# Half of the modulation's chunks moved from VectorE to TensorE, and two column groups taken in turn

## The reference, cut to what matters

```python
def rmsnorm(x, g):
    xf = x.astype(jnp.float32)
    y = xf * lax.rsqrt(jnp.mean(xf * xf, axis=-1, keepdims=True) + EPS)
    return (y * g.astype(jnp.float32)).astype(x.dtype)
...
    c_act = jax.nn.silu(c)
    for l in range(DEPTH):
        mod = c_act @ w_ada[l] + b_ada[l]
        sh1, sc1, gt1, sh2, sc2, gt2 = jnp.split(mod[:, None, :], 6, axis=-1)
        h = rmsnorm(x, g_mix[l]) * (1.0 + sc1) + sh1
        x = x + gt1 * hybrid_mixer(h, w_in[l], ...)
```

## Time and profile before

| what | value |
|---|---|
| median of three runs | 3170.58 us (3169.29 to 3181.39) |
| the profiled execution, its own time | 3177.1 us |
| its span | 3175.3 us |
| mean granted share of TensorE's clock | 0.981 |
| TensorE busy | 3067.2 us (97%) |
| VectorE busy | 2004.9 us (63%) |
| ScalarE busy | 1482.3 us (47%) |
| moved by DMA | 658.41 MB, mean 207 GB/s |

### The profile page before, as it was taken

The page is one execution under the profiler, slowest core; times in us unless marked ns, Lnnn a source line. Parts: engine busy times, 40 slices in busy tenths (PEclk is TensorE's granted clock), DMA queues, the critical chain, the costliest instruction groups (busy, mean ns, idle before and its releaser), DMA issues.

```text
span 3175.3 us, 38367 instructions
## 1 busy us (share of the span) xinstructions
PE 3067.2 (97%) x14170; PEld 2544.3 (80%) x14170; DVE 2004.9 (63%) x2098; ACT 1482.3 (47%) x1740; POOL 107.4 (3%) x206
## 2 busy tenths in 40 slices
PE   6389999999999999999999999999999999999999
PEld 5278777788888888888888888888888888888887
DVE  6879778785656556766555565646575565565564
ACT  4145445544544444555445435544445454444543
POOL 1211110100000000000000000000000000000000
PEclk9689999999999999999999999999999999999999
DMA  9878777685555555555555545555555556545555
GB/s 342 319 301 329 277 272 290 255 295 186 182 194 187 190 187 183 173 174 177 182 183 185 193 153 185 179 188 180 177 175 169 193 171 194 179 156 196 167 185 191
DMA packets 179987, 658.41 MB, mean 207 GB/s; under 512 B 20080, under 2 KB 20368, under 8 KB 179216
## 3 DMA queue, kind: packets, MB, share of 16 engines
q1 hardware_dynamic: 150992, 550.51, 51.7%
q0 software_dynamic: 28864, 106.08, 9.1%
HBM read 654.41 MB, written 2.10 MB: 207 GB/s over the span
## 4 chain that ended last, share of the span: by engine, by line
PE 94%; DVE 3%; DMA 2%; issue 1%; ACT 0%; SPq 0%; DVEq 0%; ACTq 0%
PE pg L1004 29%; PE pg L1006 29%; PE pg L1005 29%; PE pm L1039 2%; DVE R L1597 1%; DMA w_raw<-w 1%; PE pm L1058 1%; DMA R<-w_ada 1%; PE pm L1476 1%; PE pm L1071 0%; PE pm L1370 0%; PE pm L1114 0%; PE pm L1113 0%; DVE w_lo L1675 0%; PE pm L1154 0%
## 5 line engine op out<-in xcount | busy, mean ns | idle before, releaser
L1525 DVE TENSOR_TENSOR w_lo<-w_raw,w_hi 128x1024 fp32r<-128x1024 f32 x888 | 1086.2, 1225 | 974.2 <-ACT w_hi L482 969.6
L482 ACT ACTIVATE w_hi<-w_raw 128x1024 fp32r<-128x1024 f32 x888 | 941.4, 1060 | 1337.7 <-PE pg L1006 1321.6
L1004 PE MATMUL pg<-w_hi,hT_hi 128*128 128x512 f32 x3232 | 1280.2, 396 | 47.2 <-DVE w_lo L1675 34.4
L1006 PE MATMUL pg<-w_hi,hT_lo 128*128 128x512 f32 x3232 | 1265.2, 391 | 0.0
L1005 PE MATMUL pg<-w_lo,hT_hi 128*128 128x512 f32 x3232 | 1264.7, 391 | 0.0
L1004 PEld LDWEIGHTS pg<-w_hi,hT_hi 128*128 128x128 f32 x3232 | 611.6, 189 | 176.3 <-issue 42.9
L1006 PEld LDWEIGHTS pg<-w_hi,hT_lo 128*128 128x128 f32 x3232 | 610.8, 189 | 128.8
L1005 PEld LDWEIGHTS pg<-w_lo,hT_hi 128*128 128x128 f32 x3232 | 612.0, 189 | 124.2 <-issue 0.5
L1004 PE MATMUL pg<-w_hi,y_parts 128*128 128x512 f32 x864 | 337.9, 391 | 1.4 <-issue 1.4
L1006 PE MATMUL pg<-w_hi,y_parts 128*128 128x512 f32 x864 | 336.3, 389 | 0.0
L1005 PE MATMUL pg<-w_lo,y_parts 128*128 128x512 f32 x864 | 336.1, 389 | 0.0
(11 more groups left out here) (270 smaller groups left out, 1383.7 us busy)
## 6 DMA issues: line engine op xcount, KB each, us to landing
w_raw<-w SPq DMA_DIRECT2D x1028, 512.0 KB, 3.5
R<-w_ada POOLq DMA_DIRECT2D x196, 512.0 KB, 5.9
R<-mem_T SPq DMA_DIRECT2D x4, 512.0 KB, 9.4
x_rows<-x SPq DMA_DIRECT2D x1, 2048.0 KB, 20.6
R<-mem_T SPq DMA_DIRECT2D x1, 2048.0 KB, 10.2
out<-x_rows SPq DMA_DIRECT2D x4, 512.0 KB, 5.2
con_sb<-con SPq DMA_DIRECT2D x1, 1344.0 KB, 7.3
small_w_sb<-small_w POOLq DMA_DIRECT2D x2, 576.0 KB, 5.4
```

What stands on the lines that cost most here:

```text
L482: act.activation(w_hi[:, g % RING, :, :].rearrange("p c n -> p (c n)"), raw[:, g % RING, :], ACT.Copy).then_inc(hi_done, 1)
L1004: pe.matmul(out, hi, w_hi[:, slot, c, :], start=start, stop=False)
L1006: return pe.matmul(out, lo, w_hi[:, slot, c, :], start=False, stop=stop)
L1525: tt(flat(w_lo[:, g % RING, :, :]), raw[:, g % RING, :], flat(w_hi[:, g % RING, :, :]).bitcast(F32), ALU.subtract).then_inc(lo_done, 1)
```

## The change

1. In `CHUNKS` the halves 0 and 1 take turns chunk by chunk, and then the halves 2 and 3. The two shift halves (1 and 3, `PE_HALVES`) are not weighed on VectorE: TensorE multiplies each chunk with silu(c) and accumulates in `pm[3]` (`mod_sums`), beginning with the bias. Since 16 products of 8 columns are added in the bank, `ada_sums` isn't needed for them. POOL waits for the engine that used chunk i - 5.
2. Tiles 0 to 7: VectorE weighs two chunks of half 0 after each w_lo, TensorE takes two of half 1 after each tile. Tiles 8 to 23: one chunk of half 2 and one of half 3 a tile. Later halves are weighed from tile 24 on.
3. Tiles 16 to 31: x takes four tiles (input blocks 0 to 7), y four, then x the other four and y the other four.
4. The row norm stands after tile 6's share on VectorE and ScalarE instead of 9; `rows_T` stands between tiles 7 and 10, in three banks. The constants' first part (128 KB) is loaded ahead of the memory's tokens. The forget gate's product comes after tile 27. Many later places in the three programs move by one to four tiles.

```diff
+F_X, F_Y = FRONT.index("x"), FRONT.index("y")
+F_TILES = [(u, j) for u in range(F_X) for j in range(GT)]
+F_TILES += [(u, j) for first in (0, GT // 2) for u in (F_X, F_Y) for j in range(first, first + GT // 2)]
+F_TILES += [(u, j) for u in range(F_Y + 1, F_OUT) for j in range(GT)]
...
+PE_HALVES = (1, 3)
+CHUNKS = [(h, k) for a in (0, 2) for k in range(KD) for h in (a, a + 1)]
+CHUNKS += [(h, k) for h, (q, _) in enumerate(HALVES) if h > 3 for k in range(-1 if q in (2, 5) else 0, KD)]
+DVE_HALVES = [h for h in range(len(HALVES)) if h not in PE_HALVES]
...
             sp.dma_start(vec[:, :], t["vec"]).then_inc(vec_in, 16)
+            sp.dma_start(con[:, 0:2 * P], t["con"][:, 0:2 * P]).then_inc(con_in, 16)
...
                 if i >= ADA_RING:
-                    pool.wait_ge(ada_used, i - ADA_RING + 1)
+                    by_pe = CHUNKS[i - ADA_RING][0] in PE_HALVES
+                    pool.wait_ge(ada_pe if by_pe else ada_used, chunks_before(i - ADA_RING + 1, by_pe))
...
+            act.wait_ge(tile_used, 2 * GT)
             for p in range(4):
                 if p == 2:
-                    upto(22)
+                    upto(26)
                 act.wait_ge(hm_ready, p + 1)
...
+            def mod_sums(h, k):
+
+                i = chunk_at(h, k)
+                q, e = HALVES[h]
+                at = VEC["b_ada"][0] + q * KD + e * (AH // P)
+                out = pm[3][:, 0:AH // P]
+                if k == 0:
+                    if h != PE_HALVES[0]:
+                        pe.wait_ge(mod_taken, 1)
+                    pe.matmul(out, ident, vec[:, at:at + AH // P], start=True, stop=False)
+                pe.wait_ge(ada_in[i % ADA_RING], 16 * (i // ADA_RING + 1))
+                for m in range(AH // P):
+                    last = pe.matmul(out[:, m:m + 1], ada_ring[:, i % ADA_RING, m * P:(m + 1) * P],
+                                     c_act[:, k:k + 1], start=False, stop=k == KD - 1 and m == AH // P - 1)
+                last.then_inc(ada_pe, 1)
...
+            for t in range(8):
+                upto(t + 1)
+                mod_sums(1, 2 * t)
+                mod_sums(1, 2 * t + 1)
+                if t == 7:
+                    pe.wait_ge(rows_ready, 1)
+                    rows_T(0, 0, xn_1)
+                    rows_T(0, 1, xn_1)
+            for t in range(8, 16):
+                upto(t + 1)
+                mod_sums(3, t - 8)
+                if t <= 10:
+                    for q in range(2 * (t - 7), 2 * (t - 7) + 2):
+                        if q >= 3:
+                            pe.wait_ge(hf_done, q - 2)
+                        rows_T(0, q, xn_1)
+            pe.wait_ge(hf_done, GT)
+            ada_sums(0, 0)
             pe.wait_ge(hn_ready, 1)
-            pe.wait_ge(hf_done, GT)
-            transposes(mk_tok[0], (2, 3), T_ps)
-            upto(16)
-            ada_sums(0, 0)
-            ada_sums(1, 1)
-            upto(20)
+            transposes(mk_tok[0], (1, 2), T_ps)
+            for t in range(16, 24):
+                upto(t + 1)
+                mod_sums(3, t - 8)
             pe.wait_ge(mod_taken, 2)
             ada_sums(2, 0)
-            ada_sums(3, 1)
-            upto(24)
+            upto(28)
...
-            weighs = {16 + 6 + i: (4 + i // KD, i % KD) for i in range(6 * KD)}
-            weighs.update({i: (0, i) for i in range(KD)})
+            weighs = {16 + 8 + i: [(4 + i // KD, i % KD)] for i in range(6 * KD)}
+            weighs.update({i: [(0, 2 * i), (0, 2 * i + 1)] for i in range(8)})
+            weighs.update({8 + i: [(2, i)] for i in range(KD)})
...
-            upto(13)
+            upto(11)
+            take_mod(1, 3)
+            upto(14)
             mem_heads(0)
-            upto(20)
-
-            for k in range(KD):
-                weigh(1, k)
-                if k == 3:
-                    take_mod(0, 0)
-            take_mod(1, 1)
+            upto(16)
+            take_mod(0, 0)
             scale_gain(16, V("g_mix")[:, 0:8], 2)
             dve.wait_ge(hf_done, GT)
             modulated(0)
             modulated(1)
-            for k in range(2):
-                weigh(2, k)
+            upto(17)
             lower_4(P_MIX, hf_1)
             lower_4(P_MIX + 1, hf_1)
-            for k in range(2, KD):
-                weigh(2, k)
-            for k in range(KD):
-                weigh(3, k)
-                if k == 3:
-                    take_mod(2, 0)
-                if k in (4, 9):
-                    upto(21 + k // 9)
+            upto(24)
+            take_mod(2, 0)
             take_mod(3, 1)
             scale_gain(24, V("g_mix")[:, 8:16], 4)
             modulated(2)
             modulated(3)
+            upto(26)
             lower_4(P_MIX + 2, hf_1)
             lower_4(P_MIX + 3, hf_1)
```

More of the change, by code:

```diff
@@ L51 @@
 F_OUT = FRONT.index("o0")
-F_TILES = [(u, j) for u in range(F_OUT) for j in range(GT)]
+F_X, F_Y = FRONT.index("x"), FRONT.index("y")
+F_TILES = [(u, j) for u in range(F_X) for j in range(GT)]
+F_TILES += [(u, j) for first in (0, GT // 2) for u in (F_X, F_Y) for j in range(first, first + GT // 2)]
+F_TILES += [(u, j) for u in range(F_Y + 1, F_OUT) for j in range(GT)]
 F_TILES += [(F_OUT + n, j) for n in range(2) for j in range(6)]
@@ L62 @@
 HALVES = ((1, 0), (0, 0), (1, 1), (0, 1), (4, 0), (3, 0), (2, 0), (2, 1), (4, 1), (3, 1), (5, 0), (5, 1))
-CHUNKS = [(h, k) for h, (q, _) in enumerate(HALVES) for k in range(-1 if q in (2, 5) else 0, KD)]
+PE_HALVES = (1, 3)
+CHUNKS = [(h, k) for a in (0, 2) for k in range(KD) for h in (a, a + 1)]
+CHUNKS += [(h, k) for h, (q, _) in enumerate(HALVES) if h > 3 for k in range(-1 if q in (2, 5) else 0, KD)]
+DVE_HALVES = [h for h in range(len(HALVES)) if h not in PE_HALVES]
 IN2 = 15
@@ L399, in chunks_used, with chunks_before, turn @@
         def chunks_used(h):
-            return sum(1 for i, _ in CHUNKS if i <= h)
+            return sum(1 for i, _ in CHUNKS if i <= h and i not in PE_HALVES)
+        def chunks_before(i, by_pe):
+            return sum(1 for h, _ in CHUNKS[:i] if (h in PE_HALVES) == by_pe)
+        def turn(h):
+            return DVE_HALVES.index(h)
         P_MEM0, P_MIX, P_Y, P_MEM1, P_FF = 0, 4, 8, 16, 24
@@ L420, in _ @@
                 if g == 3:
-                    sp.dma_start(con[:, 0:2 * P], t["con"][:, 0:2 * P]).then_inc(con_in, 16)
                     sp.dma_start(x[:, :, :], t["x"]).then_inc(x_in, 16)
@@ L632, in _ @@
             act.activation(spl[:, 0:4], spl[:, 0:4], ACT.Ln, bias=1.0).then_inc(lam_out, 1)
-            upto(9)
+            upto(6)
             act.wait_ge(x_in, 16)
             squares(0, sq_1)
-            upto(13)
+            for q in range(GT):
+                upto(11 + q // 3)
+                rows_T(0, q, hf_1, False)
+            upto(14)
             head_std(0, 8)
-            for q in range(GT):
-                upto(14 + q // 2)
-                rows_T(0, q, hf_1, False)
-            upto(19)
-            heads_T(0, (2, 3), mk_T[:, 0, :, :], scale=V("mk_g")[:, 0:1])
-            upto(20)
+            upto(17)
+            heads_T(0, (1, 2), mk_T[:, 0, :, :], scale=V("mk_g")[:, 0:1])
+            upto(18)
+            act.wait_ge(tile_used, 2 * GT)
             for p in range(4):
                 if p == 2:
-                    upto(22)
+                    upto(26)
                 act.wait_ge(hm_ready, p + 1)
@@ L672, in _ @@
             for gate, (dst, bias) in enumerate(((GR, "ba"), (GI, "bi"))):
-                upto(40 + 3 * gate)
+                upto(43 + 3 * gate)
                 act.wait_ge(lru_ps, gate + 5)
@@ L1070, in ada_sums @@
                 for m in range(AH // P):
-                    i = pe.matmul(pm[bank][:, m:m + 1], ada_acc[h % 2][:, m * P:(m + 1) * P], ones[:, 0:1],
+                    i = pe.matmul(pm[bank][:, m:m + 1], ada_acc[turn(h) % 2][:, m * P:(m + 1) * P], ones[:, 0:1],
                                   start=True, stop=True)
                 i.then_inc(acc_read, 1)
+            def mod_sums(h, k):
[12 more added lines that the diff above has]
+                last.then_inc(ada_pe, 1)
             def broadcast(h, bank):
@@ L1078, in broadcast @@
                 for n in range(2):
-                    i = pe.matmul(pm[bank + n][:, :], ones, ada_acc[h % 2][:, n * NW:(n + 1) * NW], start=True,
+                    i = pe.matmul(pm[bank + n][:, :], ones, ada_acc[turn(h) % 2][:, n * NW:(n + 1) * NW], start=True,
                                   stop=True)
@@ L1175, in _ @@
             for gate in range(2):
-                upto(36 + 3 * gate)
+                upto(39 + 3 * gate)
                 pe.wait_ge(lru_act, 2 + 2 * gate)
@@ L1235, in _ @@
             y_T(1, o1)
-            upto(105)
+            upto(107)
             ada_sums(8, 0)
-            upto(117)
+            upto(119)
             ada_sums(9, 1)
@@ L1676, in upto @@
                        flat(w_hi[:, g % RING, :, :]).bitcast(F32), ALU.subtract).then_inc(lo_done, 1)
-                    if g in weighs:
```

(6 more changed lines are left out.)

96 lines of the change are left out of this document (47 added, 49 removed).

## The result

The changed kernel is slower: 3201.12 us, median of four runs (3196.8 to 3201.9), beside 3174.32 us for the kernel before in the same turns. The ratio is 1.0071, its 95% interval 1.0049 to 1.0093. Measured again in later turns, it was 1.0065 (1.0046 to 1.0084). By these ratios 21 to 23 us are lost (27 by the two medians), more than the 0.5% that I took for the limit of no change.

What follows compares the result with a forecast made beforehand. VectorE's 48 chunks outside the tile loop were taken to stall TensorE about 29 + 34 us. Stages summed to 216.0 us at tile 28 against 206.6, taken as +10 on the median 3170.6: 3181 us, range 3160 to 3204.

Steps and rivals of the forecast that it cites:

- likeliest case: The forecast's own case, chance 0.46: 3181 us, by itself 3172 to 3190, with tiles 0 to 7 ending at 89 us.
- the clock returns late: Rival, chance 0.27: most wide stretches of tiles 0 to 7 end before the clock rises, 11 us a tile, time 3204.
- the sum up to tile 28: Stages added until TensorE is ready for tile 28: 216.0 us against 206.6 before, 9.4 later, taken as +10.
- tiles 0 to 7: A tile and two chunks on TensorE, half the time at each clock level: 8.15 us, times 8 is 65.2.
- The wait for 3.7 us at tile 6: TensorE's earlier idle time, 39.4 to 43.1 us, as tile 6 landed late; kept at 3.7 since the transfers stay.
- The constants, 0.3 us: Loading con's 128 KB ahead of the memory tokens: 0.3 us of transfer, costed at nothing; first matmul at 20.2.
- The bank wait: In tiles 8 to 15, mod_sums(3, 0) waits for VectorE to free bank 3: 7.4 us in all, TensorE idle about 4.
- Tiles 16 to 23 and the chains: Tiles 16 to 23 with ada_sums 39.4 us; TensorE idle 6.7 us ahead of tile 16, 8.7 ahead of tile 24.
- L1195: The forget gate's product after tile 27, L1154 in the kernel before: 64 instructions of eight columns, priced at 8.65 us.
- the start of tile 28: A half-clock start of tile 28, 2.4 us, counted ahead of the mark; before, it had fallen into tile 24.
- the end of the stalls: Moving chunks off VectorE or into the tile loop removes TensorE's stalls of 29 and 34 us as such.

## Why the prediction failed in its likeliest case

The recorded range holds 3201 us, but the forecast, 3181 and no change, was 20 us too low. What came is near the price of the rival *the clock returns late* (3204), but that nearness is partly luck. The rival has tile 8 at 110 us or later, and it came at 97.7, between my own 89 and the rival's. Of the 20 us and a half, 10.4 stand in the sum up to tile 28, some 4.4 behind that mark, where I had expected no difference, and the other 6 or so lie in the medians: the profiled execution of the kernel before was 6.5 us above the median that I had used, that of the change only 0.7 above its own.

**The term that was mis-sized: tiles 0 to 7.** "About half the time at each" clock level gave 8.15 us a tile, 65.2 us for eight. They took 72.6 us without waits, 9.1 a tile (9.26 with them, (97.66 - 1.8 - 21.80) / 8), above the point of 8.9 from which I had said that the loss passes 16 us. The step that failed is the half: the level was low for about 47 of the 74 us, 63%. By the prediction's own formula 0.63 at the low level gives 8.9 us. The parts say the same: 84% of the wide matmuls at half level make 4.75 us a tile, the narrow pairs took 4.3, together 9.05. The rival's story, wide stretches cut before or just when the level returns, was the right one in kind, and its 11 us a tile were too much: what I weighed at 0.27 had its evidence in the earlier trace rows, where the level came up only late in a tile. Half the products left out gave 7 us back at tile 8, seven in eight 16, so that the products set this stage is shown. How much of it is the clock's and how much the products' own time isn't separated by a run, since the cut kernels wait for loads instead.

**The wait for 3.7 us at tile 6** did not recur as such; TensorE waited 1.1 us for a chunk and 0.4 us for w_lo of tile 6. Being slow, it hid the loads. So this term, too large by some 2.3, covered part of the other (7.4 too small), and the stage as a whole was only 5.2 us off.

**The constants, 0.3 us.** The first matmul was 1.6 us late, in the repetition 1.9; with the edit undone it came at 19.6 and 19.5. I had counted the 0.3 us of transfer only. By the chain, what the first matmul waited for is weight tile 0: issued at the same time (3.57, before 3.52), it took 15.75 us to land instead of 14.16, and 13.6 and 13.7 in the two kernels with the edit undone alone. Why it takes so much more than 0.3 us stays open. The term was too small by 1.3 to 1.6 us. What it costs at the end stays open, between nothing (all chunks on VectorE) and 6 us.

**The bank wait.** The way round is as foreseen: load 96.49 (5.98), the multiply-add 102.50 (1.28), bank free at 103.9, 7.4 us, just the sum in the prediction. TensorE came late to it, so 1.4 us of idle time instead of 4. But tiles 8 and 9 and their chunks ran at half level too, L1102 2.60 instead of 1.68; the stage cost 2.7 more.

**Tiles 16 to 23 and the chains** were right within 1 us. With one chunk a tile TensorE held the full level from tile 17 on: 4.57 us a tile, 1.68 of it narrow. **L1195** took 11.20 instead of 8.65 us. It began at the full level as in the kernel before, but the level fell after some 2 us of it (clock 1.00 from 215.3 to 217.3, 0.55 from 217.3 to 221.0) and not after 5 (189.7). This was made up at the mark by the start of tile 28, which I had counted ahead of it and which falls behind it.

**What the sum could not show** is the comparison with the other engine. The prediction priced the chunks' removal from VectorE as the end of the stalls. The runs show that the stalls were in good part due to the order: 48 chunks stood outside the tile loop, and VectorE stood idle for 41 us ahead of tile 28. Placing the chunks otherwise on VectorE gives 18 to 22 us; the change, with half of them on TensorE, costs 21 to 23. In part the stalls are VectorE's and the loads' own: with all chunks on VectorE, TensorE still stands idle for 45 us ahead of tile 28, against 70 before.

By the Trainium skill (TensorE: Matmul & The Clock Gate, Part 1: The HAM clock gate), the level follows how busy the engine has been. Busy time as the profile counts it doesn't decide here: 98% busy at a clock of 0.71 in the change, 78% busy at 0.95 with all chunks on VectorE.

## What to carry to other kernels

Before moving work to another engine, try it at another place on the same engine: ask whether the stall comes from the engine's load or from its order. Work of a few columns between wide matmuls is to be priced twice, by its own time and by the level at which it leaves the next wide stretch; don't take half the time at each level, but follow the level through one period. One trace tells the place of a gain, and repeated times its size, as soon as the place is one where the clock can fall either way.

## What the runs showed that I had not expected

- Half a tile and a chunk in turn mostly kept whichever level they had: low for 22 us, then full for 30, then, after a wait, low for 17. A whole tile and two chunks in turn changed level twice in nearly every tile.
- The clock's column read 1.00 in the kernel with half tiles in turn until 44 us, while matmul starts were 0.43 us apart. In the change it read 1.00 until 26.5 us in the same way. Ahead of the first change in the record the column is no evidence; the spacing of the starts is. This is the row of the half tiles:

```profile
22.30:44.20 21.90, 21.88 (x79) 19.61 (x79) 10.04 (x9) 8.96 (x12) 3.66 (x7) 1.00 0.87 335
```

- Tiles 60 to 67 and the work between them took 33.7 to 41.6 us from one execution to another with TensorE busy throughout. The Trainium skill (TensorE: Matmul & The Clock Gate, Part 1: The HAM clock gate) says of a kernel's start that the number of matmuls at the low level varies between runs of one kernel. Here it varies in the middle of one too: 38.5 and 41.6 us in the two executions of the change.
